# A hybrid decoder trunk: token tiles in the outer loop of the mixer output, and transposes ahead of scores in each attention step

## The reference

```
o = att @ v                       # GLA, retention: inside a chunk of tokens
o = o + q_dec @ prev              # and the state left by the chunks before
o = rms_norm(o) * silu(r)

s = q @ k.T * HD**-0.5, masked    # sliding-window attention (and MoBA,
m = max(s.max(-1), sink)          # without the sink)
p = exp(s - m); denom = p.sum(-1) + exp(sink - m)
o = p @ v / denom
```

## Time and profile before

| | |
|---|---|
| median of 3 runs | 1447.72 us (1446.3 to 1448.02) |
| profiled execution | 1447.72 us |
| its span, first to last instruction | 1445.9 us |
| mean granted TensorE clock | 0.984 of full speed |
| TensorE busy | 1380.7 us, 95% of the span |
| vector, scalar, GpSimd busy | 31%, 33%, 34% |
| chain that ended last | TensorE 78%, DMA 14%, vector 3% |

### The profile page before, as it was taken

How to read it: one execution, slowest core, us unless ns; L and a number is a source line. 1 busy time by engine, 2 the same in 40 slices (tenths; PEclk the granted TensorE clock), 3 DMA queues, 4 the chain that set the end, 5 groups by cost and what they waited for, 6 DMA issues and landing times.

```text
span 1445.9 us, 19158 instructions
## 1 busy us (share of the span) xinstructions
PE 1380.7 (95%) x7602; PEld 962.3 (67%) x7602; DVE 452.6 (31%) x1080; ACT 476.9 (33%) x839; POOL 484.7 (34%) x240
## 2 busy tenths in 40 slices
PE   7999999999999999988999999999999999998886
PEld 6889877788888633333388888777888884333333
DVE  3232644410333411211333435443103243211114
ACT  4522476632332111111253326765223311111112
POOL 2633433456650111111144342335566401111101
PEclk9999999999999999999999999999999999999999
DMA  7522222233377999999963213222243789999996
GB/s 263 186 89 88 74 73 74 74 109 131 110 249 307 356 394 420 418 420 416 391 247 99 86 61 110 73 74 73 81 160 128 257 323 391 420 420 420 420 413 266
DMA packets 136467, 331.24 MB, mean 229 GB/s; under 512 B 16629, under 2 KB 98629, under 8 KB 113848
## 3 DMA queue, kind: packets, MB, share of 16 engines
q1 hardware_dynamic: 127736, 314.29, 57.8%
q0 software_dynamic: 8640, 15.69, 2.9%
HBM read 312.17 MB, written 33.55 MB: 239 GB/s over the span
## 4 chain that ended last, share of the span: by engine, by line
PE 78%; DMA 14%; DVE 3%; SPq 2%; ACT 2%; issue 1%; POOL 0%; DVEq 0%; POOLq 0%; ACTq 0%
PE ps L583 18%; PE ps L585 17%; PE ps L584 17%; PE ps L1000 14%; DMA w<-in_w 12%; SPq L476 2%; PE ps L793 1%; PE ps L779 1%; PE ps L799 1%; DMA yb<-y_dram 1%; PE ps L736 1%; PE ps L992 1%; PE ps L898 1%; DMA raw<-in_w_in 1%; PE ps L947 1%
## 5 line engine op out<-in xcount | busy, mean ns | idle before, releaser
L583 PE MATMUL ps<-uH,ringH 128*128 128x512 f32 x704 | 275.8, 392 | 0.0
L585 PE MATMUL ps<-uH,ringL 128*128 128x512 f32 x704 | 274.2, 390 | 0.0
L584 PE MATMUL ps<-uL,ringH 128*128 128x512 f32 x704 | 274.2, 389 | 0.0
L1000 PE MATMUL ps<-w,xT 128*64 128x512 f32 x1024 | 231.1, 603 | 11.0 <-DMA w<-in_w 10.2
L1000 PEld LDWEIGHTS ps<-w,xT 128*64 128x64 f32 x1024 | 77.5, 139 | 157.1 <-issue 152.0
L1000 PE MATMUL ps<-w,hT 128*64 128x512 f32 x512 | 127.6, 644 | 31.8 <-DMA w<-in_w 19.9
L1440 POOL TENSOR_TENSOR ringL<-raw,ringH 128x2048 fp32r<-128x2048 f32 x28 | 128.6, 4601 | 80.7 <-ACT ringH L1149 80.7
L585 PEld LDWEIGHTS ps<-uH,ringL 128*128 128x128 f32 x704 | 132.2, 188 | 27.9
L583 PEld LDWEIGHTS ps<-uH,ringH 128*128 128x128 f32 x704 | 132.2, 188 | 27.4
L584 PEld LDWEIGHTS ps<-uL,ringH 128*128 128x128 f32 x704 | 132.3, 188 | 27.1
L1484 POOL TENSOR_TENSOR ringL<-raw,ringH 128x2048 fp32r<-128x2048 f32 x32 | 147.0, 4595 | 5.1 <-ACT ringH L1298 5.1
(11 more groups left out here) (281 smaller groups left out, 2094.0 us busy)
## 6 DMA issues: line engine op xcount, KB each, us to landing
w<-in_w SPq DMA_DIRECT2D x176, 1024.0 KB, 17.4
raw<-in_w_in SPq DMA_DIRECT2D x54, 1024.0 KB, 5.2
w<-in_w SPq DMA_DIRECT2D x32, 512.0 KB, 17.9
raw<-in_w_out SPq DMA_DIRECT2D x8, 1024.0 KB, 5.3
yb<-y_dram SPq DMA_DIRECT2D x8, 1024.0 KB, 15.1
braw<-in_w_branch SPq DMA_DIRECT2D x24, 256.0 KB, 4.6
h_dram<-hs SPq DMA_DIRECT2D x2, 2048.0 KB, 11.4
y_dram<-attT SPq DMA_DIRECT2D x8, 512.0 KB, 8.4
```

The costliest lines, as they stand in the source:

```text
L583: mm(o, h, rh, start=first, stop=False)
L584: mm(o, h, rl_, start=False, stop=False)
L585: return mm(o, l, rh, start=False, stop=last)
L1000: ins = mm(o[r], lhs[:, r], rhs[x], start=first, stop=last, skip_group_check=True)
```

## The change

Two edits, both in TensorE's stream. In `mix_out` the loop over token tiles becomes the outer one: for each tile the state products of all heads, then the full-size products of all heads. The start flag is set for each tile instead of for the first alone, and `mix_filled` is raised for each head at its last tile. In `step` the transposes of pair s-1 stand ahead of the scores of pair s, and the scores' wait for `probs_raw` is gone (the transposes' wait for `probs_ready` covers it).

```
@@ mix_out
-                o = [[ps[:, A[h] * 512 + t * DV:...] for h in range(HEADS)] for t in range(NT)]
                 for t in range(NT):
+                    o = [ps[:, A[h] * 512 + t * DV:A[h] * 512 + (t + 1) * DV] for h in range(HEADS)]
                     for c in ((2 * t, 2 * t + 1) if br == 0 else (t,)):
                         for h in range(HEADS):
                             if br == 0:
-                                mm(o[t][h][half_rows], qi[...], prev[r4[h], c, :], start=t == 0, ...)
+                                mm(o[h][half_rows], qi[...], prev[r4[h], c, :], start=True, ...)
                             else:
-                                mm(o[t][h], qi[r4[h], tmc(t)], prev[r4[h], t, :], start=t == 0, ...)
-                for h in range(HEADS):
-                    for t in range(NT):
-                        last = mm(o[t][h], attT[:, h, t, :], vv[:, t, DV * h:DV * (h + 1)], start=False, stop=True, ...)
-                    last.then_inc(mix_filled.h, 1)
+                                mm(o[h], qi[r4[h], tmc(t)], prev[r4[h], t, :], start=True, ...)
+                    for h in range(HEADS):
+                        last = mm(o[h], attT[:, h, t, :], vv[:, t, DV * h:DV * (h + 1)], start=False, stop=True, ...)
+                        if t == NT - 1:
+                            last.then_inc(mix_filled.h, 1)
@@ step: this block moves from ahead of the transposes to behind them
                 if s < NITEMS // 2:
                     if s == 0:
                         pe.wait_ge(mix_scaled.h, mix_scaled.at(lay, 8))
                     for n in (2 * s, 2 * s + 1):
                         win, h, t, k0, nk = item(n)
-                        if s:
-                            pe.wait_ge(probs_raw.h, probs_raw.at(lay, n - 1))
                         ...
                         mm(bank(A[n % 2], nk * P), q, k, start=True, stop=True).then_inc(scores_filled.h, 1)
```

More of the change, by code:

```diff
@@ L723, in mix_out @@
                 qi = qT if br == 0 else bT
-                o = [[ps[:, A[h] * 512 + t * DV:A[h] * 512 + (t + 1) * DV] for h in range(HEADS)] for t in range(NT)]
                 for t in range(NT):
+                    o = [ps[:, A[h] * 512 + t * DV:A[h] * 512 + (t + 1) * DV] for h in range(HEADS)]
                     for c in ((2 * t, 2 * t + 1) if br == 0 else (t,)):
@@ L729, in mix_out @@
                                 half_rows = slice(CG * (c % 2), CG * (c % 2 + 1))
-                                mm(o[t][h][half_rows], qi[r4[h], CG * c:CG * (c + 1)], prev[r4[h], c, :], start=t == 0, stop=False,
+                                mm(o[h][half_rows], qi[r4[h], CG * c:CG * (c + 1)], prev[r4[h], c, :], start=True, stop=False,
                                    skip_group_check=True)
                             else:
-                                mm(o[t][h], qi[r4[h], tmc(t)], prev[r4[h], t, :], start=t == 0, stop=False, skip_group_check=True)
-                for h in range(HEADS):
-                    for t in range(NT):
-                        last = mm(o[t][h], attT[:, h, t, :], vv[:, t, DV * h:DV * (h + 1)], start=False, stop=True,
+                                mm(o[h], qi[r4[h], tmc(t)], prev[r4[h], t, :], start=True, stop=False, skip_group_check=True)
+                    for h in range(HEADS):
+                        last = mm(o[h], attT[:, h, t, :], vv[:, t, DV * h:DV * (h + 1)], start=False, stop=True,
                                   skip_group_check=True)
-                    last.then_inc(mix_filled.h, 1)
+                        if t == NT - 1:
+                            last.then_inc(mix_filled.h, 1)
             def window_values():
@@ L801, in step @@
                         last.then_inc(probs_turned.h, 1)
+                if s < NITEMS // 2:
+                    if s == 0:
+                        pe.wait_ge(mix_scaled.h, mix_scaled.at(lay, 8))
+                    for n in (2 * s, 2 * s + 1):
+                        win, h, t, k0, nk = item(n)
+                        g = h // 2 if win else h % 2
+                        r = slice(HD * g, HD * (g + 1))
+                        keys = slice(k0 * P, (k0 + nk) * P)
+                        q, k = (swq[r, h % 2, tmc(t)], swk[r, keys]) if win else (mq[r, h // 2, tmc(t)], mk[r, h // 2, keys])
+                        mm(bank(A[n % 2], nk * P), q, k, start=True, stop=True).then_inc(scores_filled.h, 1)
             PIECES = {3: log_decay, 7: lambda: scores(0), 8: lambda: chunk_kv(0), 10: lambda: mix_out(0),
```

## The result

| | before | after |
|---|---|---|
| median, 4 runs each | 1447.01 us | 1455.73 us |
| ratio, 95% interval | | 1.0075 [1.0062, 1.0087] |
| profiled execution, span | 1445.9 us | 1454.1 us |

By these two medians the change makes the kernel 8.7 us slower; the forecast was +8.1. The ratio rests on more executions: 17 of the changed kernel are on record, the four of the table and 13 others, from 1455.4 to 1460.0 us with a median of 1458.2. It stands for +10.9 us, with an interval from +9.0 to +12.6.

A forecast was written before the change was run, and what follows sets the result against it. TensorE was taken to bound the mixer stage, so its added instruction time counts in full. Shape changes of 4.8 us in attention steps and 3.3 in output pieces sum to 8.1 on 1447.72: 1455.8 us, range 1449.5 to 1459.0.

The forecast's parts named there:

- one for one: Expert weight stream behind the mixer: a later TensorE makes it start later by the same amount.
- edit 1: Attention steps 2 to 15, transposes ahead of scores: one more shape entry each, 28 x 0.17 = 4.8 us.
- again no difference: Attention step: leaving the scores toward a full-size product costs the same as toward a transpose.
- step 1: Attention step without value products: same shapes with the transposes first, so priced at nothing.
- Edit 2: Output pieces, token tiles outermost: three more round trips between shapes per call, 3.3 us in all.
- The re-entry: Output piece, from full-size products back into the 32-row shape: seen nowhere, taken at 0.13 us, bounds 0 and 0.17.
- The late head signals: Output piece, four head signals moved into the last tile: squares and sums about 1.0 us later, hidden, costing nothing.
- The norm: Second branch's output: big product `L1694` ends at 155.1, wanted at 155.8, so hidden with 0.7 us to spare.
- The softmax: Attention step 2: last scaling of probabilities ends 0.67 us before the moved transposes would start.
- A (half-hidden switches): Shape switches partly hidden, 0.05 us each, 52 give 2.6 us: 1450.3, within 0.2%; chance 0.12.
- B (dear waits): 60 removed score waits held TensorE 0.17 us each, 10.2 us back: faster, 1445.6; chance 0.05.
- C (late probabilities): Step 2 of each layer: probabilities 2.7 us later, TensorE stands 2.0 us per layer: 1459.8; chance 0.09.

The follow-up runs named there:

- the nine kernels of the table: The kernel before, the changed kernel and seven follow-up variants, compared by mixer stretch per layer; spans from 1445.9 to 1457.3 us.
- the kernel with the waits put back: Kernel before with transposes ahead of scores, the scores' 60 waits for exponentials kept at their new place: 1451.43 us, 1.0030.
- the extra product: Kernel before plus one 64-column identity product in steps 2 to 15: between value products and scores 1460.96 us, ahead of the value products 1453.49 us.

## Why the prediction was right

**The bound.** TensorE is the bound of the mixer stage and never waits there: shown, since its list of waits is empty there, the nine kernels of the table repeat that stage to 0.01 us in both layers, and the edits add up to 0.01. That the queue follows the mixer one for one is shown for layer 0 by the first weights, 4.12 us late, which is 4.52 for the mixer less 0.47 for an earlier start of it, and 0.07 in between. That the end of the experts' stage follows too is shown only as well as the last column of the table: seven of its nine kernels lie between 1017.6 and 1018.8 while their mixers differ by 9 us. The two others have their excess at a lower granted clock.

**The number.** In the mixers the two edits cost 9.03 us, 0.9 over the forecast, nearly all of it in edit 1. The spans of the two profiled executions differ by 8.2, and that this is the forecast's 8.1 is luck: 9.03 in the mixers and 1.3 at the lower clock behind the second one, less 1.7 for a shorter experts' stage in layer 0 (224.95 us for 226.66) and 0.5 for an earlier start. None of these three is the edits' doing as far as the runs show: the first expert stage takes 224.8 to 225.1 or 226.5 to 226.7 in all ten kernels, and the kernel with the waits put back has 226.65. The ratio of all executions stands for +10.9, and the 1.9 us beyond the mixers stay unexplained. The 17 executions of the changed kernel have a mean granted clock of 0.9856, the 53 of the kernel before 0.9870; that this is the cause is not shown.

**Edit 1.** The mechanism is shown by the extra product: one more change of shape costs 0.19 to 0.20 us wherever the data stand. The term was sized at 28 x 0.17 = 4.8 and came to 5.7, just over its upper bound of 5.6. The entry from transposes into the scores was right (0.59 - 0.41 = 0.18). What the sum left out is the product behind the scores: it has 0.50 where it had 0.47 behind a transpose, and the next one follows 0.02 to 0.03 later, which I had not seen since I read the step only up to that product's start. So "again no difference" for leaving the scores toward a full-size product was wrong by that much. And step 1, priced at nothing, costs 0.03, and 0.02 more behind it.

**Edit 2.** 3.3 forecast, 3.4 measured, but partly by two errors that cancel. The re-entry, for which no row existed, was taken at 0.13 and is 0.14 in both forms: the full-size products of a GLA piece take 4.02 us in all, 3.59 before, for three re-entries. A further block of states in the GLA piece was taken at 0.19 and costs (4 x 0.30 - 0.84)/3 = 0.12, since a short block of state products runs faster than a long one. In the retention piece it was taken at 0.10 and costs (4 x 0.38 - 1.05)/3 = 0.16: between the first two groups of four in each block lie 0.16 us, between later ones 0.11, and I had spread that slow start over the long block.

**The covers.** The late head signals cost nothing. The norm was to end 0.7 us before its use, and ended 0.70 before, though both ends moved 0.2 further than thought: the norm by 1.2 us for 1.0, and its use by the 0.90 of the retention piece for 0.7. The softmax kept 0.73 us at step 2, where 0.67 was read off before.

**The rivals.** A (half-hidden switches) needs 0.05 us a switch; none was under 0.09. B (dear waits) fell with the waits put back. C (late probabilities) did not occur; even with the transposes in front of the step, TensorE's list of waits does not name them.

**The drain.** The rule of the Trainium skill's page "TensorEngine Tiling (Array Packing)", section "Key Properties", is that a change of tiling mode drains the engine. The traces agree in that every added change cost time, and the ones added with the same work cost 0.17 us on average (9.03 us for 28 + 24); that it is a drain, no trace shows. The estimate of 0.053 us for a drain, worked out in the prediction from the Trainium skill's page "TensorE: Matmul & The Clock Gate", section "Step-by-step: what each phase is for", gave 2.8 us, a third of that.

## What to carry to other kernels

Where TensorE is the bound and never idle, count the changes of tile shape in its stream, not only its products: each cost 0.09 to 0.20 us here, the length of one or two small products, and none of it shows in TensorE's list of waits. Order the small pieces so that equal shapes touch, and gather what has an odd shape into fewer, longer blocks, if a second buffer can be found. And compare kernels over a stretch without waits: it repeats to 0.01 or 0.02 us, where the intervals of the execution times are 1.3 to 2.5 us to each side.

## What the runs showed of the hardware that was not expected

Instructions of a 32-row, 64-column shape start faster at the head of a block than later: 0.30 us for 16, 0.41 for 32, 0.84 for 64, each up to the next block. So cutting the block of 64 in two cost 0.14 us, where the three cuts into four cost 0.26 each.

A full-size product costs 0.17 us when it stands between a full-size projection and the value products and 0.37 when it stands between two other shapes, though it is the same instruction on the same data.

Not every extra 0.09 us is a change of shape. The first 512-column product behind full-size transposes keeps the next one waiting for 0.32 us in place of 0.23 (177.90 to 178.22 in the kernel before), and both are full size. Why, no run here shows.
